# A two-block transformer kernel on one core: one small store issued inside an attention, and remainders, residual sums and copies in another order at two seams and in two attentions

## The chip, the core and the metric

The kernel runs on 1 core of a Trainium2 chip. The metric is the device time of one execution in microseconds (us). TensorE is called PE in the profile, VectorE DVE, ScalarE ACT, GpSimd POOL and SyncE SP.

## What is computed

The input is 256 tokens of width 1024. A first block (a gated feed-forward part, a hybrid mixer with latent attention and a short convolution, a second gated feed-forward part) is followed by a second block (two attentions, a squared-ReLU feed-forward part, a gated embedding). Only the first block's mixer and its two borders, and the second block's first attention, are touched here.

```python
mod = (einsum('bd,dn->bn', silu(c), w_ada) + b_ada)            # 72 blocks of 128 values
h = rms_norm(x, norm_w[0]) * (1 + mod[0, 1]) + mod[0, 0]
x = x + 0.5 * mod[0, 2] * swiglu(h, ...)                       # seam 1 follows
h = rms_norm(x, norm_w[1]) * (1 + mod[1, 1]) + mod[1, 0]
proj = h @ w_in                                                # latents, conv inputs, gates
...                                                            # latent attention of 8 heads, conv branch
x = x + mod[1, 2] * (merged @ w_out)                           # mod[1, 2] is the gate row; seam 2 follows
h = rms_norm(x, norm_w[2]) * (1 + mod[2, 1]) + mod[2, 0]
x = x + 0.5 * mod[2, 2] * swiglu(h, ...)
```

## The kernel before

**Weights.** All matrix weights stream through 161 units of 128x2048 numbers (1 MB each) in a ring of three slots. SP loads unit v into `raw` once the remainder of unit v-3 is made. ACT (`hi`, L1184) rounds it to `whi`, after PE has released unit v-3 (`w_used`). DVE (`lo`, L1742) makes the remainder `wlo = raw - whi` and counts `w_lo`. PE multiplies each 128-row chunk in three passes (L451 to L453: high by high, high by low, low by high) and waits for `w_lo` before a unit. `his(a, b)` and `los(a, b)` do a run of units. Unit numbers used below: 33, 34 are the first projection of the mixer (`U_C0`), 35, 36 `U_XV`, 37, 38 `U_GC`, 39, 40 `U_GB`, 41 `U_UQ`, 42 `U_UKV`, 43 to 50 the gates, 51, 52 and 53, 54 the two branches, 55 to 58 the output projection (`U_WO`).

**Order.** Nothing is scheduled at run time: the order on every engine is the order written in its block, and semaphores tie the engines together. So whatever is written ahead of an instruction on DVE or ACT delays it.

**Modulation (ada).** The 72 blocks of `mod` are dot products on DVE (`ada_block`, L1889). From block 48 on, their weights of 512 KB a block come through a ring of three: POOL issues the load of block b (L406) when block b-3 is done. `ada_some(a, b)` does blocks a to b-1.

**The gate row.** `store_gate(1)` (ACT, L1236) writes the 128x8 numbers of `mod[1, 2]` to DRAM as one row of 1024, transposed by its access pattern; `spread_gate(1)` (L1242) reads the row back to all partitions after the attention; `residual(2, ...)` uses it.

```python
act.dma_start(gate_dram[sub].rearrange("(k p) -> p k", p=P), mod[:, g:g + KD],
              allow_slow_non_contiguous=True).then_inc(sig("gate_stored"), 16)
```

**Seams.** At a seam, `residual(phase, t, n)` (DVE, L1878 and L1880) adds a half row of token tile t; `square` (ACT) sums its squares; `norm_factor` (DVE, 8 tiny dependent steps) makes the factor; `left` (ACT) and `right` (DVE) scale; PE transposes eight chunks (`turn_tile`, L490); `shifted` (ACT, L1211, L1216) applies gain and shift and rounds chunk k; `split` (DVE, L1837) makes its remainder; PE then does chunk k of the next projection (`project_first`), all of tile 0 before tile 1.

**Latent attention.** For head h: `scores` on PE, `masked_max` on DVE (L2228, L2231), `exps` on ACT (L1473, L1476), transposes on PE, a copy on ACT, values on PE, `heads_out` on DVE. Two heads are in flight; chunks of the gate and branch projections fill PE between the steps.

**Second block's first attention.** It works in the same way (`max_a`, `exps_a`, `mix_a`, `out_a`), with chunks of other projections as filling; ACT also moves two filled results out of PSUM (`scaled_tiles`, L1203) at h == 1 and h == 3, and the next filling chunks wait for that.

Of the kernel before, what the change touches and what calls it, by code (L numbers as in the profile page):

```python
# [16 lines left out]
KD = D // P  # L17
# [81 lines left out]
def build(nc, A, out):  # L99
    ctx = ExitStack()  # L100
    with ctx:
# [1075 lines left out]
        def _(act):  # L1177
# [208 lines left out]
            left(1, 0)  # L1386
            shifted(1, 0, range(6))
            square(1, 1, 1)
            shifted(1, 0, range(6, KD))
            his(U_C0 + 2, U_C0 + 3)  # L1390
# [11 lines left out]
            his(38, 40)  # L1402
            store_gate(1)
            act.wait_ge(w_used, U_XV + 2)
# [57 lines left out]
            heads_copy(0)  # L1462
            heads_copy(1)
            his(50, 51)
            for r in range(2, H):
# [17 lines left out]
            for h in range(H):  # L1483
                if h == 3:
                    act.wait_ge(w_used, U_GATE + 8)
                    copy(gates[:, :, 3 * N:4 * N], pair(YP), "gate_raw")
                act.wait_ge(sig("p_turned"), h + 1)
                if h >= 2:
                    act.wait_ge(sig("o_ready"), h - 1)
                copy(probsT[:, h % 2, :], bank(TP, h % 2)[:, 0:384], "pT_copied")  # L1490
                if h + 2 < H:
                    exps(h + 2)
                if h in (1, 3, 5):
                    his(52 + h // 2, 53 + h // 2)
            act.wait_ge(sig("o_turned"), 1)
            nc.scalar.activation(oT[0][:, 0:2, :], bank(TP, 0).rearrange("p (k s) -> p k s", k=2), ACT.Copy)\
# [111 lines left out]
            for h in range(HA):  # L1608
                act.wait_ge(sig("pa_turned"), h + 1)
                if h >= 2:  # L1610
                    act.wait_ge(sig("oa_ready"), h - 1)
                copy(paT[:, h % 2, 0:N], bank(TP, h % 2), "paT_copied")
                if h + 2 < HA:
                    exps_a(h + 2)
                else:
                    exps_b(h + 2 - HA)
                if h == 1:
                    act.wait_ge(w_used, U_ZB + 8)
                    act.wait_ge(sig("rs_class"), 16 * 4)
                    scaled_tiles(ACT.Identity, zb[:, :, 3 * N:4 * N], pair(YP, 2), "z_copied", rs_class)  # L1620
                if h == 3:
                    act.wait_ge(w_used, U_ZBH + 1)
                    scaled_tiles(ACT.Identity, zb[:, :, 4 * N:4 * N + 256], pair(YP, 2)[:, :, 0:256], "z_copied", rs_class)
                if h in (2, 4, 6):
                    his(107 + h // 2, 108 + h // 2)
# [97 lines left out]
        def _(dve):  # L1723
# [385 lines left out]
            right(1, 0)  # L2109
            split(1, 0, range(4))  # L2110
            residual(1, 1, 1, U_FFN[0] + 33, ybank, 0)
            los(34, 35)
            split(1, 0, range(4, KD))
            norm_factor(1, 1)
# [6 lines left out]
            ada_last(2, RING4)  # L2121
            los(36, 38)
            dve.wait_ge(ada_done, ADA_RING3)
# [17 lines left out]
            link(nc.vector.memset(uT[:, :, 0:2], 0.0))  # L2141
            los(38, 40)
            gate_columns(1, 1.0)
            ada_some(48, 52)
            dve.wait_ge(sig("cT_hi"), 3)
# [5 lines left out]

            los(40, 41)
            dve.wait_ge(sig("krope"), 2)
            dve.wait_ge(sig("tables"), 8)
# [10 lines left out]
            los(41, 43)  # L2165
            ada_some(52, 54)
            los(43, 44)
# [91 lines left out]
            for h in range(H):  # L2259
                if h + 2 < H:  # L2260
                    masked_max(h + 2)
                if h == 4:
                    branch_c(0)
                heads_out(h)
                if h == 0:
                    los(51, 52)
                if h in (1, 3, 5):
                    los(52 + h // 2, 53 + h // 2)
                if h == 2:
                    ada_some(60, 61)  # L2270
                if h == 6:
                    dve.wait_ge(sig("oT_hi"), 1)
                    nc.vector.tensor_tensor(oT[1][:, 0:2, :], bank(TP, 0).rearrange("p (k s) -> p k s", k=2),
                                            oT[0][:, 0:2, :].bitcast(F32), ALU.subtract).then_inc(sig("oT"), 2)
            for k in (2, 3):
                dve.wait_ge(sig("oT_hi"), k)
                nc.vector.tensor_tensor(oT[1][:, k, :], o_bank(k), oT[0][:, k, :].bitcast(F32), ALU.subtract)\
                    .then_inc(sig("oT"), 1)
            branch_c(1)
            ada_some(61, 62)  # L2280

# [20 lines left out]
            scaled_lo("mT", "mT_hi", 0, YP, mT, KD, None, 4)  # L2302
            ada_some(62, 64)
            los(57, 59)
# [6 lines left out]
            norm_factor(2, 0)  # L2311
            right(2, 0, True)
            los(60, 61)
            split(2, 0, range(1))
            residual(2, 1, 1, U_WO + 4, gtbank, 1)
            split(2, 0, range(1, 6))
            norm_factor(2, 1)
# [135 lines left out]
            for h in range(HA):  # L2453
# [6 lines left out]
                out_a(h)  # L2460
                if h == 0:
                    los(u + 12, u + 13)
# [266 lines left out]
```

## Time and profile before

| what | value |
|---|---|
| time before, median of 3 runs | 1035.51 us (1034.35 to 1035.86) |
| the profiled execution, its own time | 1037.69 us |
| its span | 1035.9 us |
| PE busy | 994.9 us, 96% of the span |
| DVE busy | 692.0 us, 67% |
| ACT busy | 515.5 us, 50% |
| mean granted PE clock | 0.989 of full |

PE is busy nearly all of the span, so a change of order can only act on the 41 us in which PE isn't busy, and on stretches at a lower granted clock, where busy PE does less. Positions below are us from the start of the span. In rows of the order of time, the square brackets give how long the engine had been idle before the instruction, and what ended the idle time.

### The profile page before, as it was taken

What the parts mean: (1) busy time and instruction counts of PE and PEld (TensorE: products, weight loads), DVE (VectorE), ACT (ScalarE), POOL (GpSimd) and SP (SyncE); (2) the same over time, 40 slices, a digit from 0 to 9 for tenths busy, and PEclk for the clock granted to TensorE, in tenths of its full rate; (3) what the DMA queues carried; (4) which work ended last, traced back from release to release, by engine and by line L of the source; (5) the groups of instructions that cost most, each with busy time, mean ns of one, the idle gap of its engine ahead of it and who ended that gap; (6) DMA issues with size and microseconds to landing.
All of it is one profiled execution on the core that took longest, in us unless ns stands there. A gap on an engine that the chain in (4) does not pass through costs nothing.

```text
span 1035.9 us, 12906 instructions
## 1 busy us (share of the span) xinstructions
PE 994.9 (96%) x4694; PEld 820.7 (79%) x4694; DVE 692.0 (67%) x1050; ACT 515.5 (50%) x645; POOL 44.2 (4%) x82
## 2 busy tenths in 40 slices
PE   7999999988799997999999999999999999999996
PEld 5878888767687885888888888888888888888875
DVE  6968877875897696774544789355566764455557
ACT  5553434474376647444344555754464644444353
POOL 0001111100100000100000030002000000000000
PEclk9999999989899999999999999999999999999999
DMA  9976999838846463975665385333335455454531
GB/s 373 414 258 252 273 380 353 290 107 191 295 171 243 161 232 115 341 276 190 175 223 183 140 326 189 136 120 129 129 115 199 177 222 201 166 200 165 199 122 41
DMA packets 40593, 219.41 MB, mean 212 GB/s; under 512 B 7616, under 2 KB 8384, under 8 KB 19558
## 3 DMA queue, kind: packets, MB, share of 16 engines
q1 hardware_dynamic: 26604, 179.66, 47.8%
q0 software_dynamic: 9104, 34.08, 10.3%
q10 hardware_dynamic: 4842, 5.09, 1.6%
q8 instruction: 27, 0.44, 0.2%
q14 instruction: 16, 0.13, 0.0%
HBM read 217.74 MB, written 3.70 MB: 214 GB/s over the span
## 4 chain that ended last, share of the span: by engine, by line
PE 78%; DVE 12%; ACT 4%; DMA 2%; issue 2%; ACTq 0%; DVEq 0%; POOLq 0%; SPq 0%
PE YP L451 12%; PE YP L453 11%; PE YP L452 11%; PE GP L451 10%; PE GP L453 10%; PE GP L452 10%; DVE wlo L1742 5%; PE TP L451 2%; PE TP L453 2%; PE TP L452 2%; DMA ada<-in_ada_t 1%; DVE arena L1898 1%; DMA raw<-in_stream 1%; DVE ada L1889 1%; PE GP L1013 1%
## 5 line engine op out<-in xcount | busy, mean ns | idle before, releaser
L1742 DVE TENSOR_TENSOR wlo<-raw,whi 128x2048 fp32r<-128x2048 f32 x158 | 360.8, 2289 | 163.2 <-ACT whi L1184 161.6
L1184 ACT ACTIVATE whi<-raw 128x2048 fp32r<-128x2048 f32 x160 | 306.2, 1917 | 260.2 <-PE YP L453 123.0
L451 PE MATMUL GP<-whi,hT 128*128 128x512 f32 x480 | 189.5, 395 | 0.5 <-DVE wlo L1742 0.5
L453 PE MATMUL GP<-whi,hT 128*128 128x512 f32 x480 | 187.1, 390 | 0.0
L452 PE MATMUL GP<-wlo,hT 128*128 128x512 f32 x480 | 186.8, 389 | 0.0
L451 PE MATMUL YP<-whi,bT 128*128 128x512 f32 x334 | 131.6, 394 | 1.1 <-issue 0.7
L451 PE MATMUL YP<-whi,hT 128*128 128x512 f32 (+1 forms) x288 | 118.2, 410 | 14.1 <-DVE wlo L1742 9.3
L453 PE MATMUL YP<-whi,bT 128*128 128x512 f32 x334 | 130.2, 390 | 0.0
L452 PE MATMUL YP<-wlo,bT 128*128 128x512 f32 x334 | 130.0, 389 | 0.0
L453 PE MATMUL YP<-whi,hT 128*128 128x512 f32 (+1 forms) x288 | 113.5, 394 | 0.0
L452 PE MATMUL YP<-wlo,hT 128*128 128x512 f32 (+1 forms) x288 | 113.3, 393 | 0.0
L453 PEld LDWEIGHTS GP<-whi,hT 128*128 128x128 f32 x480 | 90.1, 188 | 19.0
L451 PEld LDWEIGHTS GP<-whi,hT 128*128 128x128 f32 x480 | 90.2, 188 | 18.8 <-DVE wlo L1742 1.0
L452 PEld LDWEIGHTS GP<-wlo,hT 128*128 128x128 f32 x480 | 90.2, 188 | 17.9
L451 PEld LDWEIGHTS YP<-whi,hT 128*128 128x128 f32 x288 | 55.1, 191 | 29.4 <-DVE wlo L1742 13.5
L451 PEld LDWEIGHTS YP<-whi,bT 128*128 128x128 f32 x334 | 62.7, 188 | 14.9 <-issue 1.1
L453 PEld LDWEIGHTS YP<-whi,bT 128*128 128x128 f32 x334 | 62.7, 188 | 13.2
L452 PEld LDWEIGHTS YP<-wlo,bT 128*128 128x128 f32 x334 | 62.8, 188 | 12.6
L1889 DVE CUSTOM_DVE_ANT_0 ada<-ada,arena 128x1024 f32<-128x1024 f32 x48 | 57.9, 1218 | 14.2 <-DMA ada<-in_ada_t 14.2
L453 PEld LDWEIGHTS YP<-whi,hT 128*128 128x128 f32 x288 | 55.2, 192 | 11.3
L452 PEld LDWEIGHTS YP<-wlo,hT 128*128 128x128 f32 x288 | 55.3, 192 | 9.9
L451 PE MATMUL TP<-whi,hT 128*128 128x512 f32 x96 | 38.5, 401 | 5.0 <-DVE hT L1837 4.4
(325 smaller groups left out, 1116.3 us busy)
## 6 DMA issues: line engine op xcount, KB each, us to landing
raw<-in_stream SPq DMA_DIRECT2D x161, 1024.0 KB, 4.9
ada<-in_ada_t POOLq DMA_DIRECT2D x48, 512.0 KB, 6.2
arena<-in_ada_t SPq DMA_DIRECT2D x8, 1024.0 KB, 11.6
arena<-in_ada_t POOLq DMA_DIRECT2D x8, 512.0 KB, 6.2
bias_scratch<-bias_row POOLq DMA_DIRECT2D x1, 2560.0 KB, 15.4
arena<-in_b_gate ACTq DMA_DIRECT2D x2, 1024.0 KB, 7.3
ada<-bias_scratch POOLq DMA_DIRECT2D x16, 128.0 KB, 4.8
arena<-gate_rows ACTq DMA_DIRECT2D x3, 512.0 KB, 5.0
```

The source lines that it names most:

```text
L451: nc.tensor.matmul(out_ap, xT[0][:, k, tok], hi, start=start, stop=False)
L452: nc.tensor.matmul(out_ap, xT[0][:, k, tok], lo, start=False, stop=False)
L453: return nc.tensor.matmul(out_ap, xT[1][:, k, tok], hi, start=False, stop=stop)
L1013: last = nc.tensor.matmul(bank(GP, s % 2)[:, cols_], QbT[a:a + DB, hh // 2, tok(t)], KbT[a:a + DB, hh // 2, keys], start=True, stop=True)
L1184: nc.scalar.activation(whi[:, slot, :], raw[:, slot, :], ACT.Copy).then_inc(w_hi, 1)
L1742: nc.vector.tensor_tensor(wlo[:, slot, :], raw[:, slot, :], whi[:, slot, :].bitcast(F32), ALU.subtract)\
L1889: nc.vector.tensor_tensor_reduce(w, w, silu_c[0], 1.0, 0.0, ALU.mult, ALU.add, dst)\
L1898: nc.vector.tensor_tensor_reduce(w, w, c_act[:, :], 1.0, col("b_ada", n), ALU.mult, ALU.add, mod[:, n:n + 1]).then_inc(ada_done, 1)
```

## The change

Nothing is computed otherwise; instructions change places. The parts that the prediction speaks of:

```diff
@@ ACT, seam 1
-            shifted(1, 0, range(6))
+            shifted(1, 0, range(4))
             square(1, 1, 1)
-            shifted(1, 0, range(6, KD))
+            shifted(1, 0, range(4, KD))
@@ ACT, mixer
             his(38, 40)
-            store_gate(1)
...
             heads_copy(0)
             heads_copy(1)
+            store_gate(1)
             his(50, 51)
@@ ACT, latent attention
-                if h in (1, 3, 5):
+                if h in (1, 3):
                     his(52 + h // 2, 53 + h // 2)
+                if h == 6:
+                    his(54, 55)
@@ ACT, second block's first attention: exps_a(h + 2) / exps_b moved behind
   the copies out of PSUM of h == 1 and h == 3
-                if h + 2 < HA:
-                    exps_a(h + 2)
-                else:
-                    exps_b(h + 2 - HA)
                 if h == 1:
...
+                if h + 2 < HA:
+                    exps_a(h + 2)
+                else:
+                    exps_b(h + 2 - HA)
                 if h in (2, 4, 6):
@@ DVE, seam 1
             right(1, 0)
-            split(1, 0, range(4))
             residual(1, 1, 1, U_FFN[0] + 33, ybank, 0)
+            split(1, 0, range(2))
             los(34, 35)
-            split(1, 0, range(4, KD))
+            split(1, 0, range(2, KD))
@@ DVE, mixer
-            los(36, 38)
+            los(36, 37)
...
-            los(38, 40)
+            los(37, 40)
             gate_columns(1, 1.0)
-            ada_some(48, 52)
+            ada_some(48, 50)
             dve.wait_ge(sig("cT_hi"), 3)
...
             los(40, 41)
+            ada_some(50, 51)
...
             los(41, 43)
-            ada_some(52, 54)
+            ada_some(51, 54)
@@ DVE, latent attention
                     masked_max(h + 2)
+                if h == 2:
+                    los(52, 53)
+                if h == 3:
+                    ada_some(61, 62)
                 if h == 4:
                     branch_c(0)
                 heads_out(h)
-                if h in (1, 3, 5):
-                    los(52 + h // 2, 53 + h // 2)
                 if h == 2:
                     ada_some(60, 61)
+                if h == 3:
+                    los(53, 54)
                 if h == 6:
+                    los(54, 55)
...
+            ada_some(62, 63)
             branch_c(1)
-            ada_some(61, 62)
+            ada_some(63, 64)
...
-            ada_some(62, 64)
             los(57, 59)
@@ DVE, seam 2
             right(2, 0, True)
+            residual(2, 1, 1, U_WO + 4, gtbank, 1)
+            split(2, 0, range(2))
             los(60, 61)
-            split(2, 0, range(1))
-            residual(2, 1, 1, U_WO + 4, gtbank, 1)
-            split(2, 0, range(1, 6))
+            split(2, 0, range(2, 6))
@@ DVE, second block's first attention
-                if h == 0:
+                if h == 1:
                     los(u + 12, u + 13)
```

## Rows read from the trace of the kernel before

**Rows 1.** The page: PE's busy time, and the median landing of an ada load.

```profile
PE 994.9 (96%) x4694; PEld 820.7 (79%) x4694; DVE 692.0 (67%) x1050; ACT 515.5 (50%) x645; POOL 44.2 (4%) x82
...
ada<-in_ada_t POOLq DMA_DIRECT2D x48, 512.0 KB, 6.2
```

**Rows 2.** The waits of PE, whole span: us in total, times, longest us.

```profile
PE YP L451 <- DVE wlo L1742: 9.3, 2, 8.7
PE TP L451 <- DVE hT L1837: 4.4, 4, 1.7
```

**Rows 3.** Stretches: busy time of PE, PEld, DVE, ACT, POOL; clock; DMA share; GB/s.

```profile
216.00:218.00 2.00, 2.00 (x7) 1.90 (x7) 1.72 (x10) 2.00 (x4) 0.00 (x0) 0.50 0.60 152
250.00:255.00 5.00, 5.00 (x24) 4.14 (x23) 0.00 (x0) 1.92 (x1) 0.00 (x0) 1.00 1.21 39
260.00:265.00 5.00, 0.00 (x0) 0.00 (x0) 4.65 (x7) 0.00 (x0) 0.53 (x1) 0.50 0.62 223
265.00:270.00 5.00, 4.99 (x12) 3.97 (x13) 4.83 (x8) 0.00 (x0) 0.00 (x0) 0.53 0.64 219
```

**Rows 4.** Transfers issued from 240 to 265: packets of a queue; KB, us to landing.

```profile
q10 hardware_dynamic: 1040, 0.00, 2.3%
...
ada<-in_ada_t POOLq DMA_DIRECT2D x4, 512.0 KB, 14.4
gate_rows<-mod ACTq DMA_DIRECT2D x1, 4.0 KB, 14.3
```

**Rows 5.** DVE in order of time, behind its long wait.

```profile
260.35 1.23 DVE L1889 CUSTOM_DVE_ANT_0 ada<-ada,arena 128x1024 f32<-128x1024 f32 x1 [12.78 <-DMA ada<-in_ada_t]
```

**Rows 6.** PE in order of time, at unit 40.

```profile
265.01 0.80 PE L451 MATMUL YP<-whi,hT 128*128 128x512 f32 x1 [8.74 <-DVE wlo L1742]
```

**Rows 7.** Seam 1, DVE in order of time.

```profile
209.83 0.23 DVE L1836 CAST hT<-arena 128x128 fp32r<-128x128 f32 x1 [1.38 <-ACT arena L1211]
...
211.77 0.68 DVE L1878 TENSOR_TENSOR arena<-YP,arena 128x512 f32<-128x512 f32 x1
...
213.10 2.29 DVE L1742 TENSOR_TENSOR wlo<-raw,whi 128x2048 fp32r<-128x2048 f32 x1
```

**Rows 8.** Seam 1, ACT in order of time.

```profile
217.83 0.72 ACT L1197 ACTIVATE arena<-x,xs 128x512 f32<-128x512 f32 x1
```

**Rows 9.** Seam 1, PE in order of time.

```profile
215.73 0.69 PE L451 MATMUL YP<-whi,hT 128*128 128x416 f32 x1 [2.70 <-DVE hT L1837]
...
220.03 1.05 PE L490 MATMUL GP<-ident,arena 128*128 128x128 f32 x4
```

**Rows 10.** Latent attention: ACT and then DVE in order of time.

```profile
310.01 0.58 ACT L1459 ACTIVATE arena<-TP 96x512 f32<-96x512 f32 x1
...
323.40 1.90 ACT L1184 ACTIVATE whi<-raw 128x2048 fp32r<-128x2048 f32 x1
...
320.11 1.22 DVE L1889 CUSTOM_DVE_ANT_0 ada<-ada,arena 128x1024 f32<-128x1024 f32 x1
...
324.44 0.29 DVE L2228 CUSTOM_DVE_ANT_0 arena<-GP,arena 128x128 f32<-128x128 f32 x1 [3.10 <-PE GP L788]
```

**Rows 11.** Latent attention: POOL's issue of the load of block 59.

```profile
314.35 0.53 POOL L406 DMA_DIRECT2D ada<-in_ada_t  x1 [32.14 <-DVE mod L1889]
```

**Rows 12.** Before and at seam 2: DVE, then PE, in order of time.

```profile
359.85 1.23 DVE L2248 TENSOR_TENSOR arena<-YP,arena 128x1024 f32<-128x1024 f32 x1 [2.02 <-ACT arena L1503]
...
375.34 1.21 DVE L1889 CUSTOM_DVE_ANT_0 ada<-ada,arena 128x1024 f32<-128x1024 f32 x1
...
391.85 1.09 PE L490 MATMUL YP<-ident,arena 128*128 128x128 f32 x8 [1.10 <-DVE arena L1810]
```

**Rows 13.** Second block's first attention: ACT, then PE, in order of time.

```profile
675.51 0.56 ACT L1590 ACTIVATE arena<-GP,nm,rs 128x256 f32<-128x256 f32 x1 [2.81 <-DVE nm L2415]
...
676.61 1.26 ACT L1203 ACTIVATE arena<-YP,rs_class 128x512 f32<-128x512 f32 x2
...
677.92 0.39 PE L892 MATMUL YP<-whi,hT 128*128 128x256 f32 x1 [1.42 <-ACT arena L1203]
```

## The prediction, made before the kernel was run

> **What bounds the kernel.** I read the page first: PE is busy 994.9 of 1035.9 us [rows 1], so the change can only give back idle PE and slow-clocked PE. The waits of PE name what there is: 9.3 us for weight remainders (`wlo`), 8.7 of them in one wait, and 4.4 us in four waits at seam 2 [rows 2]. The order of time places the long one: PE stands still 8.74 us ahead of unit 40, until 265.01 [rows 6]. The stretches show the price behind it: PE does 24 matmuls in 250 to 255, none in 260 to 265, and only 12 in 265 to 270, where the granted clock is 0.53, nearly the lower of its two levels (1.2 of 2.4 GHz) [rows 3].
>
> The reader should follow that wait back. Unit 40's remainder is late because DVE, which works strictly in written order, stood 12.78 us until 260.35 for the weights of ada block 51 [rows 5]. That block has nothing to do with unit 40; it is merely written ahead of it, the fourth of `ada_some(48, 52)`, and its load could only be issued when block 48 was done. The load took 14.4 us where the usual one takes 6.2 [rows 1, 4]. In the same stretch lies `store_gate(1)`: 4 KB, but over a thousand packets on its queue, 14.3 us to landing [rows 4], while in 250 to 255 the DMA engines count as fully busy at 39 GB/s [rows 3]. So two causes stack: the small store stops the loads, and the written order lets a stopped load hold PE.
>
> **The change, part by part.** I walk forward, always asking when PE gets what it waits for; gains at PE add up because between these places PE has no idle time to absorb them.
>
> *Seam 1.* DVE idles 1.38 us until 209.83, waiting for ACT [rows 7]; the last half row's sum (two steps from 211.77 to 213.10, 1.33 us) now fits in that hole for nothing. Splits of chunks 0 and 1 end at about 210.8, so the remainder of unit 34 starts 2.3 us earlier (210.8 for 213.10) and ends at 213.0. PE pays a new wait of some 1.5 us ahead of chunk 2, instead of 2.70 us ahead of chunk 4 [rows 9], and gets through tile 0 by 216, paced by ACT (0.69 us a chunk). Then `norm_factor` for tile 1 starts behind chunk 7's split at 215.2; 1.7 us of small steps later, and behind ACT's rounding of unit 35 and two bias copies, ACT's `left` can start at about 217.5 (before 217.83 [rows 8]), and PE can transpose at 218.1 instead of 220.03 [rows 9]; before, the lower clock (0.50 [rows 3]) had kept it on tile 0 until then. From there ACT sets the pace as before: 1.9 us gained. Moving the remainder of unit 37 behind the latents removes 2.2 us ahead of these; PE's wait for the latents goes, and a wait of about 0.3 us for unit 37 takes its place. Together 2.2 us. Bounds: 0.5, if the two short waits keep the clock low until 224 and PE falls behind ACT; 3.0, if the clock never falls.
>
> *The stall.* Ahead of unit 40, DVE now has only blocks 48 and 49, whose weights are there. Counting on from seam 1: unit 37's remainder is ready at 237.4, 38 and 39 at 241.8, blocks 48 and 49 at 244.4, `cT` at 245.7. Unit 40 is loaded once 37's remainder is made, 7.6 us of loading make it 245, so its remainder is ready at 249; PE wants it at 253.8. Cover of almost 5 us. Block 51 comes behind unit 42's remainder, near 258, seven or more microseconds after its load would land. So all 8.74 us go. The slow clock goes with them: 12 matmuls instead of 24 in 5 us, 0.21 to 0.23 us each, is 2.3 to 2.5 us; I take 2.3. Sum 11.0; bounds 8.7 (the clock falls anyway) and 11.2.
>
> *The store in its new place.* It isn't gone: it is now issued behind `heads_copy(1)`, which ends at 310.6 [rows 10], all positions here on the clock of the kernel before. Its 14.3 us then cover 310.6 to 324.9. What flies in that time? Unit 51, issued 309.2, wanted by ACT at 323.40 [rows 10]: it starts ahead of the store and has 12 us. Units 52 and 53 have slack of over 5 us behind the store's end. Block 59's weights, issued at 314.35 [rows 11], are wanted at 320.11 [rows 10]. Without the store they land in 3.6 to 6.2 us, in time. With it: block 51 was issued 1.8 us behind the store and landed 1.8 us behind its landing, so I expect block 59 at 326.6; at worst 14.4 us after its issue, 328.8. DVE, in order, then does `masked_max(2)` at about 327.8 instead of 324.44. That lets two links of the attention slip: PE's values of heads 1 and 2 by 0 and 1.0 us. Behind them is `los(52, 53)`, which now stands behind `masked_max(4)`, so DVE has that maximum ready at 334.1 rather than 336.2 and the delay stops growing. At the other end, unit 54's rounding moved from h == 5 to h == 6 frees 0.5 us that PE lost there. Net cost 0.5 us; bounds -0.5 (it lands in time, and the half microsecond is kept) and +5 (block 59 at 328.8 or later, or unit 51 late too, 1 us of PE for each us, through four heads).
>
> The Trainium skill ("DMA: Bandwidth & Descriptors", "Queues, rings and completion order") says that each DMA engine takes packets from its queues in turn. By it a 512 KB load of few large packets should pass between the store's thousand small ones in a fraction of 14 us: block 59 would be in time, and the attention would cost nothing. The trace disagrees, since block 51 landed only behind the store [rows 4], so I don't use it. The same page ("Rules for kernel authors") says that a non-contiguous last dimension makes a descriptor for each element; by that rule, the 1040 packets for 1024 numbers [rows 4] agree, and they come along to the new place.
>
> *Ada blocks 62 and 63* leave the way ahead of seam 2: one is done in the 2.02 us that DVE idled until 359.85, the other takes block 61's place, which now lies in a hole of the attention; at 375.34 two blocks, 2.3 us, go from ahead of units 57 and 58 [rows 12].
>
> *Seam 2.* So `residual(2, 0, 1)` is no longer late by DVE, but bound by PE's tile (385.8): 1.3 us earlier, and the first wait of 1.10 us [rows 12] goes. The last half row's sum needs PE's last chunk (392.3 now), then chunks 0 and 1, then unit 60's remainder (394.8 to 397.0). PE waits some 2.0 us for its first chunk and 1.5 for chunk 2, which is what it had, but `norm_factor` for tile 1 starts at 397.9 instead of 399.25, and tile 1's transposes are at 402.1 instead of 403.6. 1.5 us, out of the 5.5 that the five waits held [rows 2, 12]; bounds 0 and 2.2.
>
> *Second block's attention.* ACT's copy at h == 1 stood behind `exps_a(3)`, which idled 2.81 us for its maximum; it ran at 676.61, PE waited 1.42 us for it [rows 13]. The PSUM data is ready at 674.2: copied first, it ends at 675.5, before PE gets there at 676.5. `exps_a(3)` can start then, as before, because unit 107's remainder has left the way of its maximum. 1.4 us; bounds 0 and 1.4. At h == 3 the same exchange delays `exps_a(5)` by 1 us, which has a whole head of cover.
>
> **Sum.** 2.2 + 11.0 - 0.5 + 1.5 + 1.4 = 15.6 us: the profiled execution (span 1035.9; its own time 1037.69) goes to a span of 1020.3, and the median of the runs, 0.4 us under that span, to 1019.9. I say 1020.
>
> **Rivals.** (a) *The store bites in the attention.* For it: the order of DVE is as strict there, and block 59 stands ahead of the maxima of all later heads. Against it: two heads are in flight and filling chunks cover PE. Price 3 to 6 us more: 1023 to 1026. (b) *The seams give nothing*: each removed wait reappears one step later (ACT's 0.69 us a chunk, unit 34 or 60). For it: at both seams a new wait of 1.5 us stands beside the old one's place. 1035.5 - 11.0 - 1.4 + 0.5 = 1023.6. (c) *By the page's rule of taking turns* the small store costs the attention nothing: every term stays, the 0.5 turns around, 1019. That alone is within the main case's range. (d) *The store isn't what delayed block 51*, three ada loads and a unit together were. Then moving it does nothing, but the reordering alone still takes block 51 from ahead of unit 40: the stall goes, no new one comes, 1019.4. (e) *Slower than before:* the store holds block 59 and units 51 and 52 as it held unit 42 and block 51, DVE and ACT both stand, and PE runs dry for longer than the 16 us gained elsewhere. It decides from a landing of block 59 at about 340, 15 us behind the store's end; nothing that I saw landed so late. 1037.
>
> **Chances.** Main case with (c) and (d) 0.62; (a) 0.22; (b) 0.11, (e) 0.02, anything between (b) and no change 0.03. All but the last two are far over 0.2% (2.1 us), about what a measurement of this kernel can tell from no change: faster 0.96, same 0.02, slower 0.02. Range: the best bounds give 3.0 + 11.2 + 0.5 + 2.2 + 1.4 = 18.3, 1017.2; (a) reaches to 1026. Range 1017 to 1026; the main case's own is 1018 to 1022.5.
>
> **What would show it.** PE's wait of 8.7 us for `wlo` gone and no stretch at the lower clock near it; the store's landing still about 14 us, now from about 297 on the new clock; behind it DVE's wait for block 59 of 4 to 7 us; tile 1's transposes at seam 1 near 218; PE's waits at seam 2 down to about 4 us; the wait of 1.42 us gone. I am wrong if PE waits more than 3 us in the attention, if unit 37 or 40 is late, or if the clock falls at a new place.

## The result, and the profile after

The changed kernel takes 1022.12 us in the median of four runs (1021.36 to 1022.56), beside 1035.68 us for the kernel before (1034.35 to 1036.58, four runs): ratio 0.9873, 95% interval 0.9861 to 0.9885. That is 13.6 us less, against 15.5 forecast. A later comparison with nine runs of the kernel before gave 0.9871 (0.9856 to 0.9886). The span of its profiled execution is 1020.0 us, where 1020.3 was forecast. The 15.6 us of the forecast were a difference to a profiled execution that was itself 2 us slower than the median of its runs, and were then taken off the median as well. Much of what follows is about these 2 us.

The page of the changed kernel, and PE's waits in the order of their size:

```profile
PE 990.8 (97%) x4694; PEld 817.6 (80%) x4694; DVE 692.0 (68%) x1050; ACT 515.2 (51%) x645; POOL 44.1 (4%) x82
```

```profile
PE TP L451 <- DVE hT L1839: 3.1, 3, 2.1
...
PE YP L820 <- ACT arena L1245: 1.4, 2, 0.8
...
PE YP L451 <- DVE wlo L1744: 0.5, 1, 0.5
```

Beside [rows 2], the 9.3 us for remainders are down to 0.5, seam 2's 4.4 us to 3.1, and a new wait of 1.4 us has come, in the attention. Where PE had stood still, it is now busy throughout from 244 to 259, at full clock, while the transfers run at 403, 321 and 211 GB/s in the three stretches of 5 us instead of 39. The middle one (columns as in [rows 3]):

```profile
249.00:254.00 5.00, 5.00 (x24) 4.14 (x23) 4.37 (x5) 1.48 (x2) 0.53 (x1) 1.00 0.85 321
```

The store took its own trouble along. The transfers issued between 290 and 315, where it now lies, answer to [rows 4]: the same 1040 packets and 14.8 us, and now the units' loads are held too.

```profile
q10 hardware_dynamic: 1040, 0.00, 2.3%
...
raw<-in_stream SPq DMA_DIRECT2D x3, 1024.0 KB, 12.8
ada<-in_ada_t POOLq DMA_DIRECT2D x3, 512.0 KB, 13.4
gate_rows<-mod ACTq DMA_DIRECT2D x1, 4.0 KB, 14.8
```

What that does in the attention, from POOL's issue of the load to DVE and PE, in the order of time:

```profile
300.66 0.53 POOL L406 DMA_DIRECT2D ada<-in_ada_t  x1 [31.62 <-DVE mod L1891]
...
314.08 1.22 DVE L1891 CUSTOM_DVE_ANT_0 ada<-ada,arena 128x1024 f32<-128x1024 f32 x1 [7.59 <-DMA ada<-in_ada_t]
...
317.52 0.43 PE L820 MATMUL YP<-arena 128*128 128x64 f32 x2 [0.81 <-ACT arena L1245]
...
322.85 0.43 PE L820 MATMUL YP<-arena 128*128 128x64 f32 x2 [0.64 <-ACT arena L1245]
```

The load of block 59 is issued at 300.66 and there at 314.08. DVE stands for it 7.59 us, the maxima of head 2 come behind it, ACT stands 4.14 us for them, and PE waits 0.81 and 0.64 us for ACT's copies. Seam 1, in PE's order of time, answers to [rows 9]:

```profile
213.10 0.45 PE L451 MATMUL YP<-whi,hT 128*128 128x416 f32 x1 [1.40 <-DVE hT L1839]
...
217.91 0.66 PE L490 MATMUL GP<-ident,arena 128*128 128x128 f32 x4 [1.18 <-ACT arena L1197]
```

At seam 2 PE waits 2.06, 0.43 and 0.62 us, which are the 3.1 us above.

**A ledger by stretches.** To see where time goes I measure on PE between marks that every version has: the transposes of tile 0 at seam 1 (208.83 before), the first transposes of the short convolution (L696; 239.07), the 1.16 us in which PE's sequencer issues behind chunk 4 (320.42), the first chunk of seam 2's projection (395.00), and the last waited-for chunk of that seam (405.25). Lengths in us:

| profiled execution | seam 1 | mixer | latent attention | seam 2 | rest | span |
|---|---|---|---|---|---|---|
| before | 30.24 | 81.35 | 74.58 | 10.25 | 630.65 | 1035.9 |
| after | 27.46 | 70.63 | 74.98 | 9.27 | 629.03 | 1020.0 |
| gain | 2.78 | 10.72 | -0.40 | 0.98 | 1.62 | 15.9 |

0.20 us of the 15.9 lies ahead of the first mark.

### The profile page after: what moved, and what is told of

Same layout as the page of the kernel before. It is cut to its first block, busy times and chain, and to the rows that moved or that the text cites. A ratio compares the mean times of both kernels' runs of the same rounds, so it can differ in the third digit from the quotient of the medians.

```text
span 1020.0 us, 12906 instructions
## 1 busy us (share of the span) xinstructions
PE 990.8 (97%) x4694; PEld 817.6 (80%) x4694; DVE 692.0 (68%) x1050; ACT 515.2 (51%) x645; POOL 44.1 (4%) x82
## 4 chain that ended last, share of the span: by engine, by line
PE 79%; DVE 12%; ACT 4%; DMA 2%; issue 1%; ACTq 0%; DVEq 0%; POOLq 0%; SPq 0%
PE YP L451 11%; PE YP L453 11%; PE YP L452 11%; PE GP L451 11%; PE GP L453 10%; PE GP L452 10%; DVE wlo L1744 4%; PE TP L451 2%; PE TP L452 2%; PE TP L453 2%; DVE arena L1900 1%; DMA ada<-in_ada_t 1%; DMA raw<-in_stream 1%; ACT whi L1184 1%; PE GP L1013 1%
## 5 line engine op out<-in xcount | busy, mean ns | idle before, releaser
L451 PE MATMUL YP<-whi,hT 128*128 128x512 f32 (+1 forms) x288 | 116.3, 404 | 4.6 <-DVE hT L1839 2.7
L453 PE MATMUL YP<-whi,hT 128*128 128x512 f32 (+1 forms) x288 | 111.9, 389 | 0.0
L451 PEld LDWEIGHTS YP<-whi,bT 128*128 128x128 f32 x334 | 62.7, 188 | 14.8 <-issue 1.1
L451 PEld LDWEIGHTS YP<-whi,hT 128*128 128x128 f32 x288 | 54.1, 188 | 19.2 <-DVE hT L1839 3.8
L453 PEld LDWEIGHTS YP<-whi,hT 128*128 128x128 f32 x288 | 54.0, 188 | 11.0
## 6 DMA issues: line engine op xcount, KB each, us to landing
bias_scratch<-bias_row POOLq DMA_DIRECT2D x1, 2560.0 KB, 14.3
```

The costliest lines, as they stand in the source:

```text
L451: nc.tensor.matmul(out_ap, xT[0][:, k, tok], hi, start=start, stop=False)
L453: return nc.tensor.matmul(out_ap, xT[1][:, k, tok], hi, start=False, stop=stop)
```

## The experiments

Twelve further runs were made, in three groups; a group shares the runs of the kernel before. Timed results first, then the same ledger. The two kernels with pieces of 32 bytes store the gate values in another order, so their output is another: they measure the store and aren't kernels to use. The ratio isn't always that of the two medians; where they differ, the ratio with its interval decides (the second block's attention alone: median 1.85 us lower, ratio 0.9994).

| kernel | median us (runs) | before, same group | ratio, 95% interval |
|---|---|---|---|
| store only | 1032.57 (5) | 1037.33 | 0.9954 (0.9940 to 0.9968) |
| mixer order only | 1031.84 (5) | 1037.33 | 0.9942 (0.9929 to 0.9956) |
| changed, store in old place | 1026.36 (4) | 1037.33 | 0.9885 (0.9867 to 0.9902) |
| changed, block 59 late | 1022.27 (5) | 1037.33 | 0.9847 (0.9834 to 0.9861) |
| seam 1 only | 1034.94 (12) | 1035.44 | 0.9998 (0.9988 to 1.0008) |
| seam 2 only | 1035.75 (12) | 1035.44 | 1.0006 (0.9997 to 1.0015) |
| second block's attention only | 1033.59 (12) | 1035.44 | 0.9994 (0.9982 to 1.0006) |
| latent attention's order only | 1033.68 (11) | 1035.44 | 0.9980 (0.9968 to 0.9992) |
| changed, again | 1021.60 (4) | 1035.12 | 0.9871 (0.9856 to 0.9886) |
| changed, block 59 late, again | 1020.78 (4) | 1035.12 | 0.9864 (0.9849 to 0.9879) |
| changed, gate row in pieces of 32 bytes | 1020.42 (4) | 1035.12 | 0.9856 (0.9841 to 0.9871) |
| before, gate row in pieces of 32 bytes | 1026.28 (5) | 1035.12 | 0.9915 (0.9902 to 0.9929) |

| profiled execution | seam 1 | mixer | latent attention | seam 2 | rest | span |
|---|---|---|---|---|---|---|
| store only | 28.61 | 70.67 | 80.93 | 10.25 | 630.70 | 1030.5 |
| mixer order only | 29.56 | 75.69 | 74.60 | 10.27 | 630.83 | 1030.5 |
| changed, store in old place | 27.47 | 75.80 | 73.03 | 10.92 | 629.17 | 1026.1 |
| changed, block 59 late | 27.42 | 72.95 | 73.06 | 9.27 | 629.06 | 1020.6 |
| seam 1 only | 28.63 | 81.35 | 74.58 | 10.25 | 630.84 | 1034.9 |
| seam 2 only | 28.61 | 79.18 | 75.28 | 9.28 | 630.65 | 1032.1 |
| second block's attention only | 29.34 | 79.43 | 74.59 | 10.25 | 629.14 | 1031.5 |
| latent attention's order only | 29.51 | 79.73 | 72.32 | 10.25 | 630.78 | 1031.7 |
| changed, again | 27.79 | 70.64 | 73.20 | 9.25 | 629.09 | 1019.2 |
| changed, block 59 late, again | 27.73 | 70.68 | 73.03 | 9.25 | 629.03 | 1018.5 |
| changed, 32-byte pieces | 27.43 | 71.47 | 73.07 | 11.13 | 629.07 | 1021.5 |
| before, 32-byte pieces | 28.62 | 71.28 | 74.58 | 10.25 | 630.73 | 1024.7 |

The columns are to be read downwards: a stretch that an edit doesn't touch shows how far it varies by itself. The mixer as it is in the kernel before takes 81.35 us in two executions and 79.2 to 79.7 in three others, seam 1 as it is there 28.61 to 30.24 in six. Single edits worth less than 2 us can't be told by whole times here; the stretches can tell them.

**1. The store alone.** Against the kernel before:

```diff
             his(38, 40)
-            store_gate(1)
...
             heads_copy(0)
             heads_copy(1)
+            store_gate(1)
             his(50, 51)
```

> The kernel before, with the store of the gate row moved into the attention and nothing else changed. Theory (the store stops the loads, the written order lets a stopped load hold PE; two stacked causes, either enough by itself): block 51's load lands in 6 to 8 us, PE's wait ahead of unit 40 shrinks from 8.7 us to at most 1 us, and the slow-clocked stretch goes. In the attention the store covers block 59's load: DVE stands there for 5 to 8 us, and since unit 52's remainder is still made at h == 1, PE loses 1 to 3 us. Sum 1035.5 - 10.3 + 2 = about 1027. Rival 1 (the three ada loads and a unit together made block 51 late, not the store): block 51 still takes 12 us or more and the time stays above 1033. Rival 2 (a store among loads costs nothing by taking turns): no wait of DVE in the attention, 1025.

The stall is gone with this edit alone: the mixer takes 70.67 us, what the whole change makes of it (70.63). DVE's wait for block 51, still written ahead of unit 40, is 3.49 us (12.78 in [rows 5]). But the old order of the latent attention pays for the store dearly, 80.93 us instead of 74.58, where 1 to 3 us were expected; that is why the kernel takes 1032.57 us and not 1027:

```profile
319.25 1.22 DVE L1889 CUSTOM_DVE_ANT_0 ada<-ada,arena 128x1024 f32<-128x1024 f32 x1 [10.86 <-DMA ada<-in_ada_t]
...
322.69 0.43 PE L820 MATMUL YP<-arena 128*128 128x64 f32 x2 [4.07 <-ACT arena L1245]
```

This is rival (a) in full: 6.35 us, in the order of before. Behind the wait of 4.07 us the granted clock was at 0.50 from 324 to 326.

**2. The mixer's order alone**, the store where it was:

```diff
-            los(36, 38)
+            los(36, 37)
...
-            los(38, 40)
+            los(37, 40)
             gate_columns(1, 1.0)
-            ada_some(48, 52)
+            ada_some(48, 50)
...
             los(40, 41)
+            ada_some(50, 51)
...
-            ada_some(52, 54)
+            ada_some(51, 54)
```

> The kernel before, with only the order of DVE in the mixer changed (remainder of unit 37 behind the latents; blocks 48, 49 ahead of the latents' remainders, 50 behind unit 40's, 51 to 53 behind unit 42's); the store of the gate row stays in its old place. Theory: the store still takes 14 us and block 51 still lands some 14 us after its issue, but nothing that PE needs stands behind it by then: PE's wait of 8.7 us goes and so does the slow clock, the attention stays as it was; about 11.2 + 0.3 less than 1035.5, so 1024. Rival (the store must move, its flood also holds units 42 and 43): PE waits 3 us or more at units 42 or 43, time 1027 or more.

The mixer takes 75.69 us: of the stall only about half goes, and 1031.84 us stand where 1024 was expected. The rival had the cause right, the store holds the units too (ACT stands 7.79 us for one of them, until 266.62), but not the form: PE has three waits of 1.65, 1.30 and 1.04 us instead of one of 3 us, and the granted clock stays at full speed in this mixer. The next run shows the same with all other edits in place.

**3. The changed kernel with the store in its old place.**

```diff
             his(38, 40)
+            store_gate(1)
...
             heads_copy(1)
-            store_gate(1)
```

> The changed kernel with the store of the gate row back in its old place. Theory: the new place costs PE 1 us in the attention (DVE stood 7.59 us for block 59); the old place, with blocks 51 to 53 now behind unit 42's remainder, is covered: block 51 would land at about 258.2 where DVE wants it at 258.0, unit 42 at about 254 where ACT wants it at 253.8. So 1 us below the changed kernel, 1021. Rival (moving the store was needed too): blocks 51 to 53 and units 42, 43 are late together and PE waits for unit 43 or 44; 1024 or more, with the slow clock back after a long wait.

75.80 us in the mixer, 5.2 more than the changed kernel; 1026.36 us in all, where the theory said 1021 and the rival 1024 or more. ACT, then PE, in the order of time:

```profile
258.35 1.92 ACT L1184 ACTIVATE whi<-raw 128x2048 fp32r<-128x2048 f32 x1 [6.92 <-DMA raw<-in_stream]
265.37 1.91 ACT L1184 ACTIVATE whi<-raw 128x2048 fp32r<-128x2048 f32 x1 [5.10 <-DMA raw<-in_stream]
...
268.25 0.50 PE L451 MATMUL YP<-whi,bT 128*128 128x512 f32 x1 [2.35 <-ACT arena L1245]
...
270.38 0.47 PE L451 MATMUL YP<-whi,hT 128*128 128x512 f32 x1 [0.48 <-DVE wlo L1744]
...
277.40 0.50 PE L451 MATMUL YP<-whi,hT 128*128 128x512 f32 x1 [1.31 <-DVE wlo L1744]
```

Block 51 is out of unit 40's way, but the store (19.5 us to landing here) also holds the weight stream: ACT waits 6.92 us for one unit and 5.10 us for the next, its copy of a result behind them is late, and PE waits 4.1 us in all. The granted clock stays full here, so the rival's slow clock didn't come. What was issued just behind the store was late, weights as well as ada blocks; the order only decided who showed it.

**4. The changed kernel with block 59 one head later.**

```diff
-            ada_some(58, 60)
+            ada_some(58, 59)
...
             for h in range(H):
...
+                if h == 1:
+                    ada_some(59, 60)
```

> The changed kernel with block 59 done at h == 1 of the latent attention, behind heads_out, instead of ahead of head 0. Theory: its load, stopped by the store, was the only thing that cost PE time in the attention, through masked_max(2) and the copies behind it; now it has landed when DVE comes to it. DVE's wait of 7.59 us goes, PE's waits for copies of 0.81 and 0.64 us go, and from the first heads_turn to the first merged_turn PE takes 57.1 to 57.6 us (57.6 before the change, 58.6 after it): 1.0 to 1.5 us below the changed kernel, about 1021. Rival (the later maxima are late because the new order of units 52 and 54 costs DVE or ACT time there): PE's waits stay, the time is that of the changed kernel, 1022.

The waits in the attention are gone (73.06 us, where the changed kernel had 74.98), so the rival falls, but the median is that of the changed kernel: a wait of 1.77 us for unit 44 stands in the mixer, where the two kernels don't differ: there DVE waited 3.37 and 1.27 us for blocks 54 and 55, against 0.91 and 0.75 in the changed kernel. That is how far the landing of two loads varies from one execution to another.

**5 to 8. One group of edits each, on the kernel before.** Seam 1 only (the last half row's sum ahead of the splits, unit 34 behind two of them, and ACT's `square`):

```diff
             right(1, 0)
-            split(1, 0, range(4))
             residual(1, 1, 1, U_FFN[0] + 33, ybank, 0)
+            split(1, 0, range(2))
             los(34, 35)
-            split(1, 0, range(4, KD))
+            split(1, 0, range(2, KD))
```

> The kernel before with the new order at seam 1 alone (last half row's sum ahead of the splits, unit 34's remainder behind chunk 1, chunk 4 and 5 of ACT behind the squares). Theory: tile 1's transposes start 1.9 us earlier, and everything behind shifts, the store and the stall with it, since the store is issued when DVE has gone through what lies ahead: 1.9 us less, 1033.6. Rival (the stall swallows it, since its end is set by the store alone and the seam's gain is waited away): PE's wait at unit 40 grows by the 1.9 us, time unchanged at 1035.5.

Seam 2 only:

```diff
             right(2, 0, True)
+            residual(2, 1, 1, U_WO + 4, gtbank, 1)
+            split(2, 0, range(2))
             los(60, 61)
-            split(2, 0, range(1))
-            residual(2, 1, 1, U_WO + 4, gtbank, 1)
-            split(2, 0, range(1, 6))
+            split(2, 0, range(2, 6))
```

> The kernel before with the new order at seam 2 alone; ada blocks 62 and 63 still stand ahead of units 57 and 58. Theory: the gain of 1.6 us at seam 2 came for the most part from the ada blocks leaving the way, as PE's first wait of 1.10 us did; the order alone gives at most 0.5 us: 1035.0 to 1035.5. Rival (the order of the last half row's sum and unit 60 is what counts): 1.3 us or more, 1034.2 or less.

The second block's attention only (`exps` behind the copies out of PSUM, one remainder from h == 0 to h == 1):

```diff
-                if h + 2 < HA:
-                    exps_a(h + 2)
-                else:
-                    exps_b(h + 2 - HA)
                 if h == 1:
...
+                if h + 2 < HA:
+                    exps_a(h + 2)
...
-                if h == 0:
+                if h == 1:
                     los(u + 12, u + 13)
```

> The kernel before with only the second block's first attention changed (copies out of PSUM ahead of the exponentials on ACT, unit 107's remainder at h == 1 on DVE). Theory: PE's wait of 1.42 us at the first filling chunk behind the copy goes and nothing comes in its place: 1034.1. Rival: the exponentials of heads 3 and 5, now later, make PE wait one head on; 1035.5.

The order in the latent attention only (remainders of units 52 to 54, rounding of unit 54, blocks 61 to 63), the store in its old place:

```diff
+                if h == 2:
+                    los(52, 53)
+                if h == 3:
+                    ada_some(61, 62)
...
-                if h in (1, 3, 5):
-                    los(52 + h // 2, 53 + h // 2)
...
+                if h == 3:
+                    los(53, 54)
                 if h == 6:
+                    los(54, 55)
...
+            ada_some(62, 63)
             branch_c(1)
-            ada_some(61, 62)
+            ada_some(63, 64)
...
-            ada_some(62, 64)
```

> The kernel before with only the order in the latent attention changed (units 52 to 54, blocks 61 to 63), the store in its old place and seam 2's order as before. Theory: PE's wait of 0.53 us for a copy at head 6 goes, and so does its wait of 1.10 us ahead of seam 2's first transposes, since blocks 62 and 63 have left the way: 1.0 to 1.6 us less, 1034.2. Rival (the seam is bound by the last half row's sum, so an earlier start is waited away there): 0.5 us less, 1035.0.

By whole times, only the last is told from no change. The stretches say more. *Seam 1:* 28.63 us in the one profiled execution, no less than the shortest of the old order (28.61) and 1.6 less than the longest (30.24). The further 1.2 us down to 27.4 come only in the kernels that also have the remainder of unit 37 behind the latents; the six with both are within 27.42 to 27.79, so the two together take out most of the variation. What seam 1 gives is not kept in this run: PE next waits at unit 40 for a load (8.32 us), and the mixer takes 81.35 us. One execution doesn't tell how much of this wait the seam's gain added. *Seam 2:* the first chunk comes 0.70 us later (75.28 for 74.58) and the seam is 0.97 shorter (9.28 for 10.25), 0.3 us in sum. *The second block's attention:* 629.14 us against 630.65 to 630.84, 1.6 us, and 629.03 to 629.17 in all six other profiled kernels that have the edit: small, but the surest term of all. *The latent attention:* 72.32 for 74.58 us, 2.3 us where I had counted half a microsecond. Three waits of PE go: the 1.10 us ahead of seam 2 [rows 12], with the moved ada blocks, and 0.53 and 0.30 us for ACT's copies in the attention.

**9 and 10. The changed kernel again, beside the one with block 59 later.**

> The changed kernel itself once more, as the yardstick of the three others on this chip. If its gain lies in the order of the work alone, it stands to the kernel before as it did (0.9873), some 13 us faster. Its profile should show tile 0's transposes to the first short-convolution transpose in 27.5 us, from there to the idle 1.16 us behind chunk 4 in 70.6 to 73 us (the upper end where blocks 54 and 55 land late ahead of unit 44), and from there to the last wait of seam 2 in 84.3 us.

> The changed kernel with ada block 59 done at head 1 instead of ahead of head 0, now beside the changed kernel on the same chip. Theory: the late landing of block 59 behind the store costs the changed kernel 1.9 us in the attention (two waits of 0.81 and 0.64 us, and slow-clocked PE behind them), so this one is 1.9 us faster than the changed kernel in the median. Rival: DVE has to do the block somewhere, and the time comes back one head later: no difference.

The list of PE's waits in the changed kernel's second profile has none in the attention. Its store landed in 13.1 us, and DVE stood 5.79 us for block 59 instead of 7.59:

```profile
313.22 1.22 DVE L1891 CUSTOM_DVE_ANT_0 ada<-ada,arena 128x1024 f32<-128x1024 f32 x1 [5.79 <-DMA ada<-in_ada_t]
```

The stretch is 73.20 us for 74.98: 1.80 us less of DVE's wait, 1.78 us less of PE's time. So about 5.8 us are covered by the two heads in flight (73.03 to 73.07 us where the block is waited for at most 0.4 us), and between these two executions PE pays for the rest one for one. The slow-clocked PE that the second expectation names isn't there: the granted clock of the changed kernel was 1.00 in all of this stretch, and of its 1.9 us the list of waits shows 1.4. Putting block 59 later takes the exposure away, but in the median it brought 0.8 us, within the runs' own spread: not shown to be faster.

**11 and 12. The same 4 KB in fewer packets**, in the changed kernel and in the kernel before:

```diff
-                act.dma_start(gate_dram[sub].rearrange("(k p) -> p k", p=P), mod[:, g:g + KD],
+                row = gate_dram[sub].rearrange("(p k) -> p k", p=P) if sub == 1 else gate_dram[sub].rearrange("(k p) -> p k", p=P)
+                act.dma_start(row, mod[:, g:g + KD],
```

> The changed kernel, its gate row stored in the order in which it lies in the 128 partitions: the same 4 KB in the same place, but 32 bytes in one piece for each partition instead of 4 bytes (the gate values then stand in another order in the row, so the output is another). Theory, the packets hold the loads: the store lands in 2 to 4 us instead of 14.8, block 59 is in time, PE's waits for the copies of probabilities go, and the kernel is 1.9 us faster than the changed one. Rival, the bytes' way to DRAM and back or other loads hold block 59: its landing stays late, and the time is that of the changed kernel.

> The kernel before with the same one edit: the gate row stored in 32-byte pieces (other order of its values, so another output), still ahead of block 51 and unit 40, all orders as before. Theory, the thousand packets alone delay block 51: PE's wait of 8.7 us at unit 40 goes with its slow clock, as it did when the store alone was moved, and the attention isn't touched: 9 to 11 us faster than the kernel before, about 1026. Rival, three ada loads and a unit in flight together delay block 51: the wait stays above 5 us and the time at 1033 or more.

In the kernel before, this edit alone takes 8.8 us (ratio 0.9915), where 9 to 11 were expected, with every order as it was and the store ahead of block 51. DVE's wait for this block is 4.12 us, and PE's at unit 40 is gone. Transfers issued from 240 to 265, as in [rows 4], then a stretch; the first line is the queue of the ada loads, which in the kernel before reads 559, 2.06, 57.9% (packets, MB, share of the engines' time):

```profile
q0 software_dynamic: 576, 2.10, 23.2%
q10 hardware_dynamic: 144, 0.00, 0.3%
...
raw<-in_stream SPq DMA_DIRECT2D x5, 1024.0 KB, 6.0
ada<-in_ada_t POOLq DMA_DIRECT2D x5, 512.0 KB, 5.8
gate_rows<-mod ACTq DMA_DIRECT2D x1, 4.0 KB, 6.4
```

```profile
250.00:255.00 5.00, 5.00 (x23) 3.89 (x21) 4.52 (x6) 1.62 (x1) 0.53 (x1) 1.00 0.67 261
```

144 packets instead of 1040, the loads of ada blocks at 5.8 us instead of 14.4, 261 GB/s in the stretch that had 39, and 71.28 us for the mixer. That settles which part of the store did the harm: not its 4 KB, nor its place in ACT's order by itself, but that it went in a thousand pieces of 4 bytes. Whether it is the number of the packets or the small size of each isn't separated, since the edit changes both. In the changed kernel the store lands in 5.0 us (2 to 4 expected), block 59 is in time and the attention takes 73.07 us; what the median gained over the changed kernel (1.2 us, the ranges overlap) stays unproven, and in the profiled execution seam 2 took it back: its clock fell for longer, and the stretch is 11.13 us instead of 9.25.

## Why the prediction was right, and where it was not

**The number** was right because its largest term had the right cause, the store, and the right place; two smaller errors in the sum cancelled, and a third, in what the sum was subtracted from, didn't. That the sum came so near to the difference of the two profiles (15.6 for 15.9) is in part luck: by averages it is 14.3.

*The stall: 11.0 forecast, 10.7 between the two profiles, 9.6 on the average.* Five profiled executions have the mixer's old order and the old store: PE's wait at unit 40 was 8.74, 8.32, 7.14, 7.25 and 6.76 us, mean 7.6, and the stretch from its end to the mark 55.41, 55.79, 54.80, 54.96 and 55.74, mean 55.3, where it is 53.4 with no slow clock (70.63 less the 17.2 us ahead of the wait). So the clock costs 1.9 (2.3 in the forecast) and the wait 7.6. The 8.74 us on which I built [rows 6] was the longest of five. In the 5 us behind the end of the wait, the granted clock was 0.53, 0.50, 0.65, 0.62 and 0.50. The third of these, seam 2 only, beside the 12 matmuls in [rows 3]:

```profile
262.09:267.09 5.00, 5.00 (x15) 4.02 (x16) 4.83 (x8) 0.00 (x0) 0.00 (x0) 0.65 0.64 230
```

*Which part removes the stall* was wrong. I wrote that two causes stack and that, were the store innocent, "the reordering alone still takes block 51 from ahead of unit 40: the stall goes, no new one comes". Moving the store alone brings the mixer to 70.67 us; the new order alone brings it to 75.7; both, to 70.63. Rival (d) falls, since moving the store alone and cutting it into fewer pieces alone each end the stall, and with it falls the belief that the order was enough. What failed in my reasoning: I worked out a "cover of almost 5 us" for unit 40 by usual loading times, which holds once the store is gone, and never asked when units 42 and 43 would land with the store still there, in a stretch of which [rows 3, 4] show that what is issued behind it lands late.

*The rule of taking turns*, which I had set aside, stays aside: rival (c) asked for block 59 in time behind the store, and DVE waited for it 7.59, 5.79 and 10.86 us in three executions. By the Trainium skill's other rule ("DMA: Bandwidth & Descriptors", "Rules for kernel authors"), that a non-contiguous last dimension makes one descriptor for each element and is to be rearranged, the trace agrees: 1040 packets for 1024 elements, and 144 for 128 pieces of 32 bytes. In the kernel before, following it was worth 8.8 us for one line. The row then stands in another order, and what it costs to put that right, where the row is read back, was not measured.

*The store in its new place: -0.5 forecast, with seam 2's 1.5 that is 1.0; together 0.6 and 2.4 measured in two profiles of the changed kernel.* The mechanism came as described: landing 14.8 us, DVE's wait for block 59 within the 4 to 7 us foretold, or just over. The size is the sum of two things that I took together and mis-sized: the new order gives 2.3 us by itself (72.32 for 74.58), 1.1 of which I had counted under seam 2, and block 59 takes back nothing or 1.8 us, by where its landing falls against a cover of about 5.8 us. In the old order the same store cost 6.35 us (experiment 1). So the larger part of what the reordering gives here is that the store's cost stays small, and that I hadn't priced. Why the block landed 21.4 us behind the store's issue there (319.25 less 297.84), and 18.0 and 16.2 us in the changed kernel, is open: one execution each, and counted from the store's own landing it was 6.8, 3.2 and 3.1 us.

*Seam 1: 2.2 forecast; 2.8 between the two profiles; 1.6 on the average* of six old (29.16) and six new (27.55). Transposes of tile 1 "near 218" came at 217.91, the wait for unit 37 "of about 0.3 us" was 0.29 us. The old seam was longest where the clock was low behind its wait of 2.70 us [rows 3, 9]; the new one took 27.79 and 27.73 us in two executions with a low clock on tile 0 (0.50 from 212 to 216 in the changed kernel's second profile), against 27.4 without it.

*Seam 2: 1.5 forecast, about 1.0 in its own stretch.* PE's waits for `hT` there are 3.1 us instead of 4.4. They are 4.1 in the two kernels with the new seam whose clock stayed full there (block 59 late, and seam 2 only), so 1.0 us of that difference is only slow matmuls in place of waiting. The removal of the wait of 1.10 us [rows 12] shows in the latent attention's stretch, and it is the moved ada blocks that do it, since with seam 2's edit alone that wait stays (1.11 us).

*The second block's attention: 1.4 forecast, 1.6 measured.*

*The clock* did fall at a new place, for a short stretch at seam 2, which I had named as a sign of error. The new order isn't needed for it: it also fell there, to 0.50, with the old seam in two runs (store only, seam 1 only). The changed kernel, columns as before:

```profile
382.00:386.00 4.00, 3.56 (x10) 2.36 (x9) 3.84 (x11) 3.84 (x11) 0.00 (x0) 0.57 0.21 25
```

It cost nothing there in the changed kernel (9.27 and 9.25 us with it, 9.27 without it in the kernel of experiment 4), because PE's next step waits for DVE anyway. Where it lasted longer, 6 to 7 us instead of 3 to 4 (the changed kernel with the store in its old place, and with 32-byte pieces), the seam took 10.92 and 11.13 us.

**The sum again, from averages:** seam 1 1.6, mixer 9.6, attention and seam 2 together 0.6 and 2.4, mean 1.5, rest 1.6: 14.3 us. From this goes what a late landing of blocks 54 and 55 costs in some executions: 2.3 and 0.8 us in the mixer of two of the five profiled kernels with the new order and without the old store in it, 0.6 on the average. 13.7, where 13.5 and 13.6 were timed. The forecast's 15.6 matched the profiles' 15.9, and was 2 us too much for the medians: the profiled execution of before had the longest wait at unit 40 and the longest seam 1 of all that were profiled, and a sum made against it promises all of that back. Of the 14.3 us, 9.6 are the stall, which moving the store alone also removes; the rest is order.

## What to carry to other kernels

Count the packets of a small transfer, not its bytes: where a stretch shows the DMA engines full at a tenth or a fifth of the rate around it, look for the one small transfer in it, and try to make it contiguous before any reordering. Where several loads fly through such a stretch, none of them may be given its usual landing, and moving one victim out of the way shows the next. And when the profiled execution is slower than the median of the runs, expect of each wait and of each slow-clocked stretch in it less than it shows: profile the kernel before more than once.

## What the hardware showed that I had not expected

A store of 4 KB in 1040 packets held most loads that were issued behind it, on other queues, to 10 to 18 us (median landings of ada blocks 14.4 in the kernel before, 13.4 in the changed one, 15.7 with the store moved alone), and itself took 13.1 to 19.5 us in twelve executions; the same 4 KB in 144 packets took 5.0 and 6.4 us, and the loads around it 5.0 to 6.0 in the median. The store's own packets account for 2.3% of the engines' time between 240 and 265. It is the packets of the ada loads that stand open for longer: 57.9% of that time for 2.06 MB, and 23.2% for 2.10 MB beside the store in fewer pieces. By which mechanism the store does this, no run here shows. The loads weren't simply queued behind it either: a unit issued beside it at about 244 landed in 12.2 us, some 2 us ahead of the store.

The price of a stall isn't one number: behind waits of 6.8 to 8.7 us at the same place stood 1.4 to 2.4 us of slow matmuls (2.0, 2.4, 1.4, 1.5 and 2.3 for waits of 8.74, 8.32, 7.14, 7.25 and 6.76 us), and it doesn't follow the length of the wait. To compare executions, the stretch has to be laid from the end of the wait; between fixed marks at 265 and 270 the same five clocks read 0.53, 0.59, 0.95, 0.87 and 0.70, mostly because the wait ended up to 2.9 us earlier.
